# Two operand planes of a two-block model moved by 16 bytes in SBUF: normalised input from 32 to 16 into 256, feed-forward activations from 32 to 48

## The chip, the cores and the metric

One core of a Trainium2 chip runs the whole program; everything is fp32 and enters the matmuls as fp32r (fp32 data that TensorE takes in one pass). The metric is the device time of one execution in microseconds: the median of three runs.

## The reference

Two blocks on 256 tokens of width 1,024, one after the other. In shape:

```python
h = x
h = h + short_conv_mixer(rms_norm(h, ...), ...)                      # 1024 -> 3072 -> 1024
h = h + conv_ffn(rms_norm(h, ffn_norm[0]), w_up, conv_w, w_down)     # first feed-forward
k, v, k_rope = shared_latent_kv(h, ...)
h = h + mla_attention(rms_norm(h, ...), ...)
h = h + conv_ffn(rms_norm(h, ffn_norm[1]), w_up, conv_w, w_down)     # second feed-forward
x = rms_norm(h, final_norm)
# second block: modulated norm, bidirectional gated linear attention with a context
# of 256 tokens, then sqrelu MLP 1024 -> 4096 -> 1024
def conv_ffn(x_n, w_up, conv_w, w_down):                             # d_ff = 2816
    g, u = split(causal_dwconv(x_n @ w_up, conv_w), 2)
    return (silu(g) * u) @ w_down
```

## The kernel before

Activations lie transposed: partitions are 128 features, a chunk of 256 columns is the tokens. A plane such as `xhi` is 8 chunks side by side. For accuracy each operand of a large product is split in two fp32r planes, `hi` (rounded) and `lo` (the rest), and each block of 128x128 weights costs three matmuls of 128x256 into one PSUM bank: `whi` with `hi`, `whi` with `lo`, `wlo` with `hi` (lines L507, L508, L511 of `units`; L486, L487, L490 where a stage follows its input chunk by chunk; L605, L606, L611 for the first two units; L915 to L917 in the linear attention's output).

The weights stream through a ring of four slots of 512 KB: SP loads `raw`, ACT rounds it to `whi` (L1018), DVE subtracts to `wlo` (L1551), PE uses both as the stationary operand. The order is written out by hand for each engine, and semaphores (`slots_done`, `pe_units`, `tile_read`, `x_ready`, `y_ready`) tie them together.

Which plane a stage multiplies:

- `xhi`, `xlo` (one buffer `x2`): the normalised input of the mixer, of both feed-forwards' up projections, of the key/value latents, and of most products of the second block. In its MLP's up projection L510 takes `xhi` and `xlo` in one matmul of 512 columns and L511 follows with 256. In `moving` (L539 to L541) the roles are exchanged: x is stationary, and 512 columns of weights move.
- `yhi`, `ylo`: the mixer's product (8 chunks) and the feed-forwards' activations (22 chunks) before the down projection.
- `mhi`, `mlo`: the MLP's activations; `ohi`, `olo`: attention; `uhi`, `ulo`: four units of the MLP; `zhi`, `zlo`: the modulated context, which is moving operand in one unit (24 matmuls) and stationary in `moving`.

`sb` allocates SBUF buffers one behind another, sizes given in fp32 columns, each rounded up to 32 bytes; `stage.close()` gives the space back to the next buffers. Adding up the sizes, and with the ring at 0 into 256 bytes (`ring_pad` sees to that), the places into 256 are:

| buffer | bytes into 256 |
|---|---|
| raw, whi, wlo | 0 |
| x2 | 32 |
| yhi, ylo, m2, ohi, olo, khi, klo, chi, clo, uhi, ulo, sums_r | 32 |
| zhi, zlo, gates_hi, gates_lo | 0 |
| U | 32 |
| cv, sil, prod, side | 64 |

All these buffers' slices that a matmul reads start whole multiples of 256 bytes further on. `line_pad`, `z_pad` and `sums_pad` hold nothing; `x_held` and `down_held` only keep the space of x2 and of the feed-forward's buffers. `U` holds four results of 256 columns with two zero columns ahead of each, so that DVE's taps of the causal convolution (L1593, L1599) read it at 4 and 0 bytes, and L1695 and L1064 write and read it at 8. ACT writes `xhi` (L1102 and others) and `yhi` (L1060, L1150); DVE writes `xlo` (L1573 and others) and `ylo` (L1687, L1839).

Of the kernel before, what the change touches and what calls it, by code (L numbers as in the profile page):

```python
# [17 lines left out]
F32 = mybir.dt.float32  # L18
F32R = mybir.dt.float32r
# [5 lines left out]
T = 256  # L25
D = 1024
DC = D // P
FF = 2816
FC = FF // P
# [150 lines left out]
def program(nc, stream, xT, ctxT, vec, cst, rot, wa2, crow, out):  # L180
    ctx = ExitStack()

    def sb(name, cols, dt=F32, stack=ctx, rows=P):
        return stack.enter_context(nc.sbuf_tensor(name, [rows, cols], dt))

    with ctx:
# [20 lines left out]
        ee = sb("ee", 4 * GH)  # L207
        state = sb("state", 2 * GH * T)

        sb("line_pad", 32)  # L210
        stage = ExitStack()
        x2 = sb("x2", 2 * DC * T, F32R, stage)
        xhi, xlo = x2[:, 0:DC * T], x2[:, DC * T:2 * DC * T]
        stage.close()
        stage = ExitStack()
        csq_c = sb("csq_c", DC * T, F32, stage)
        stage.close()
        sb("x_held", 2 * DC * T)
        stage = ExitStack()
        yhi = sb("yhi", FC * T, F32R, stage)  # L220
        ylo = sb("ylo", FC * T, F32R, stage)
        U = sb("U", 4 * (T + 2), F32, stage)
        cv = sb("cv", 4 * T, F32, stage)
        sil = sb("sil", 2 * T, F32, stage)
# [2 lines left out]
        stage = ExitStack()  # L227
# [2 lines left out]
        stage.close()  # L230
        EARLY = 2 * HEADS * T + HEADS * T + HP * T + HEADS * T + 2 * T + 2 * D + 4 * RQ * T + 4 * RK * T + 6 * T + 3 * 3 * P + 24
        stage = ExitStack()
        sb("down_held", 2 * FC * T + 4 * (T + 2) + 8 * T, F32, stage)
        side = sb("side", SIDE * D, F32, stage)
        stage.close()
        stage = ExitStack()
# [24 lines left out]
        stage = ExitStack()  # L261
# [8 lines left out]
        stage = ExitStack()  # L270
# [22 lines left out]
        stage = ExitStack()  # L293
# [5 lines left out]
        stage = ExitStack()  # L299
# [2115 lines left out]
```

How the kernel before makes its waits and increments, by code:

```python
    def take(self, sem, by=1):  # L142
        self.n[sem.name] = self.n.get(sem.name, 0) + by
        self.eng.wait_ge(sem, self.value(sem))
# [6 lines left out]
    def again(self, sem, back=0):  # L152
        if self.n.get(sem.name, 0) - back > 0:
            self.eng.wait_ge(sem, self.value(sem, -back))
# [214 lines left out]
        @block.sync  # L370
# [1 line left out]
            def load_group(first, done):  # L372
                for j in range(RING):
                    sp.wait_ge(slots_done, done + (j + 1))
                    sp.dma_start(raw[:, j * D:(j + 1) * D], stream[first + j]).then_inc(raw_ready[j], 16)
# [15 lines left out]
            def load_next(p):  # L391
                sp.wait_ge(slots_done, p - RING + 1)
                sp.dma_start(raw[:, p % RING * D:(p % RING + 1) * D], stream[p]).then_inc(raw_ready[p % RING], 16)
# [11 lines left out]
            def load_down(first, last):  # L405
                for p in range(first, last):
                    load_next(p)
                    kind, u = ORDER[p]
                    if kind == "w" and u in SIDE_BEHIND:
                        s = SIDE_BEHIND[u]
                        if s >= SIDE:
                            sp.wait_ge(side_done, s - SIDE + 1)
                        sp.dma_start(side[:, s % SIDE * D:(s % SIDE + 1) * D], stream[POSITIONS + s])\
                            .then_inc(side_ready[s % SIDE], 16)
# [13 lines left out]
                sp.wait_ge(ev("out_chunk"), n + 1)  # L429
                sp.dma_start(out[:, first * T:last * T], h[:, first * T:last * T]).then_inc(ev("stored"), 16)
            sp.wait_ge(ev("stored"), 16 * len(OUT_PARTS))
```

## Time and profile before

| | |
|---|---|
| median of 3 runs (lowest, highest) | 937.57 us (937.36, 937.75) |
| the profiled execution's own time | 937.42 us |
| its span | 935.6 us, 19,755 instructions |
| PE, weight loads, DVE, ACT busy | 923.4, 879.5, 800.4, 565.6 us |
| granted TensorE clock, mean | 0.997 |
| read from HBM | 193.76 MB, 208 GB/s over the span |

PE stands for the matmuls, PEld for the weight loads that run beside them, DVE and ACT for VectorE and ScalarE; a q behind the name means the engine's sequencer. A matmul's listed duration runs from its start to its modelled end, and the next one starts long before that end: how fast PE works is read from the distance between starts in the timeline.

### The profile page before, as it was taken

The page shows a single profiled execution, that of the slowest core. Times are in us where ns is not written, and L with a number is a line of the kernel's source. Part 1 is how long each engine was busy: PE and PEld are TensorE (multiplying, and loading weights), DVE is VectorE, ACT ScalarE, POOL GpSimd, SP SyncE. Part 2 cuts the span into 40 slices and gives each one's busy share as a digit, 9 for nine tenths or more (in the row PEclk, how much of TensorE's full clock was granted, in tenths as well). Part 3 has the DMA queues.
Part 4 walks back from the last instruction along what each step waited for, and adds up shares of the span by engine and source line. Part 5 has one row for each costly group of instructions (what it writes and reads, how often), then busy time and mean ns, then how long its engine had stood idle before and what let it go on. Part 6 is the DMA issues. An engine that isn't in the chain of part 4 may idle for free.

```text
span 935.6 us, 19755 instructions
## 1 busy us (share of the span) xinstructions
PE 923.4 (99%) x6944; PEld 879.5 (94%) x6944; DVE 800.4 (86%) x1335; ACT 565.6 (60%) x935; POOL 1.8 (0%) x8
## 2 busy tenths in 40 slices
PE   9999999999999999999999999999999999999997
PEld 8999999999999899999999999988899988888886
DVE  6999899999989888899999997956878989886553
ACT  6645666666455566766666555978433667774442
POOL 0000000000000000000000000000000000000000
PEclk9999999999999999999999999999999999999998
DMA  8777575557776555555557765564674348776561
GB/s 298 258 260 231 183 276 200 193 181 275 250 271 215 164 184 173 181 186 196 184 192 274 243 251 187 174 226 157 214 263 154 134 153 265 234 231 222 184 198 45
DMA packets 53877, 195.55 MB, mean 209 GB/s; under 512 B 6110, under 2 KB 6366, under 8 KB 53696
## 3 DMA queue, kind: packets, MB, share of 16 engines
q1 hardware_dynamic: 53680, 193.78, 62.0%
q10 hardware_dynamic: 144, 1.05, 0.3%
q8 instruction: 35, 0.57, 0.2%
q14 instruction: 18, 0.15, 0.0%
HBM read 193.76 MB, written 1.05 MB: 208 GB/s over the span
## 4 chain that ended last, share of the span: by engine, by line
PE 87%; DVE 8%; ACT 2%; issue 1%; DMA 0%; DVEq 0%; SPq 0%; ACTq 0%
PE ps L511 24%; PE ps L507 19%; PE ps L508 19%; PE ps L510 10%; DVE wlo L1551 3%; PE ps L539 1%; PE ps L540 1%; PE ps L541 1%; ACT whi L1018 1%; PE ps L821 1%; DVE a L2040 1%; PE ps L660 1%; PE ps L661 0%; PE ps L662 0%; PE ps L685 0%
## 5 line engine op out<-in xcount | busy, mean ns | idle before, releaser
L1551 DVE TENSOR_TENSOR wlo<-raw,whi 128x1024 fp32r<-128x1024 f32 x303 | 366.7, 1219 | 66.3 <-ACT whi L1018 65.2
L1018 ACT ACTIVATE whi<-raw 128x1024 fp32r<-128x1024 f32 x303 | 316.9, 1052 | 88.4 <-PE ps L511 58.8
L511 PE MATMUL ps<-x,wlo 128*128 128x256 f32 x1288 | 360.0, 280 | 0.0
L507 PE MATMUL ps<-x,whi 128*128 128x256 f32 x1064 | 299.1, 281 | 0.2 <-DVE wlo L1551 0.2
L508 PE MATMUL ps<-x,whi 128*128 128x256 f32 x1064 | 296.9, 279 | 0.0
L511 PEld LDWEIGHTS ps<-x,wlo 128*128 128x128 f32 x1288 | 242.3, 188 | 0.0
L507 PEld LDWEIGHTS ps<-x,whi 128*128 128x128 f32 x1064 | 200.0, 188 | 1.0 <-issue 0.5
L508 PEld LDWEIGHTS ps<-x,whi 128*128 128x128 f32 x1064 | 200.0, 188 | 0.6 <-issue 0.5
L507 PE MATMUL ps<-yhi,whi 128*128 128x256 f32 x400 | 111.6, 279 | 0.0
L511 PE MATMUL ps<-yhi,wlo 128*128 128x256 f32 x400 | 111.6, 279 | 0.0
L508 PE MATMUL ps<-ylo,whi 128*128 128x256 f32 x400 | 111.6, 279 | 0.0
L1064 ACT ACTIVATE cv<-U,vt 128x256 f32<-128x256 f32 x88 | 44.9, 511 | 84.0 <-DVE U L1695 84.0
L510 PE MATMUL ps<-x,whi 128*128 128x512 f32 x224 | 78.1, 391 | 1.1 <-DVE mr L2244 0.7
L510 PE MATMUL ps<-m,whi 128*128 128x512 f32 x224 | 77.7, 390 | 0.0
L507 PEld LDWEIGHTS ps<-yhi,whi 128*128 128x128 f32 x400 | 75.2, 188 | 0.0
L508 PEld LDWEIGHTS ps<-ylo,whi 128*128 128x128 f32 x400 | 75.2, 188 | 0.0
L511 PEld LDWEIGHTS ps<-yhi,wlo 128*128 128x128 f32 x400 | 75.2, 188 | 0.0
L511 PE MATMUL ps<-m,wlo 128*128 128x256 f32 x256 | 72.1, 282 | 0.0
L510 PEld LDWEIGHTS ps<-x,whi 128*128 128x128 f32 x224 | 42.0, 188 | 10.6 <-DVE wlo L1551 1.0
L510 PEld LDWEIGHTS ps<-m,whi 128*128 128x128 f32 x224 | 42.0, 188 | 8.8
L511 PEld LDWEIGHTS ps<-m,wlo 128*128 128x128 f32 x256 | 48.4, 189 | 0.0
L1593 DVE SCALAR_TENSOR_TENSOR cv<-U,vt,cv 128x256 f32<-128x256 f32 x96 | 45.9, 478 | 0.6 <-ACT cv L1164 0.6
(336 smaller groups left out, 1478.9 us busy)
## 6 DMA issues: line engine op xcount, KB each, us to landing
raw<-stream SPq DMA_DIRECT2D x343, 512.0 KB, 4.2
side<-stream SPq DMA_DIRECT2D x16, 512.0 KB, 5.1
h<-xT SPq DMA_DIRECT2D x2, 512.0 KB, 5.9
c<-ctxT ACTq DMA_DIRECT2D x1, 1024.0 KB, 7.0
out<-h SPq DMA_DIRECT2D x4, 256.0 KB, 2.5
ct<-cst SPq DMA_DIRECT2D x1, 898.5 KB
rt_tab<-rot SPq DMA_DIRECT2D x1, 768.0 KB
state<-crow SPq DMA_DIRECT2D x1, 512.0 KB, 6.9
```

The costliest lines, as they stand in the source:

```text
L507: pe.matmul(dst, whi[:, w], at(hi, k), start=(k == 0), stop=False)
L508: pe.matmul(dst, whi[:, w], at(lo, k), start=False, stop=False)
L510: pe.matmul(ps[t % lag][:, :], whi[:, w], halves_of(both, k), start=(k == 0), stop=False)
L511: last = pe.matmul(dst, wlo[:, w], at(hi, k), start=False, stop=(k == K - 1))
L539: pe.matmul(dst, hi[:, tok], whi[:, w], start=first, stop=False)
L540: pe.matmul(dst, lo[:, tok], whi[:, w], start=False, stop=False)
L541: last = pe.matmul(dst, hi[:, tok], wlo[:, w], start=False, stop=final)
L660: pe.matmul(dst, whi[:, w], at(chi, k), start=(k == 0), stop=False)
L1018: c.sig(act.activation(whi[:, s * D:(s + 1) * D], raw[:, r * D:(r + 1) * D], ACT.Copy), hi_ready)
L1064: c.sig(act.activation(at(cv, j), U[:, j * (T + 2) + 2:(j + 1) * (T + 2)], ACT.Copy, scale=vt_col(i * 12 + (base + 3 * j + 2))), tap_ready)
L1551: c.sig(dve.tensor_tensor(wlo[:, w], raw[:, r], whi[:, w], ALU.subtract), slots_done)
L1593: c.sig(dve.scalar_tensor_tensor(out=at(cv, j), in0=U[:, o + 1:o + T + 1], scalar=w1, in1=at(cv, j), op0=ALU.mult, op1=ALU.add), seq_dve)
```

## The change

x2 gets 8 columns more and the program uses it from column 4 on; `line_pad` is 8 columns smaller, so x2's own start falls from 32 to 0 and the planes start at 16. `x_held` is 8 columns larger, so all that follows keeps its place. yhi and ylo become two parts of one buffer y2, used from column 4 on as well: they start at 48. U, cv, sil, prod and side come 32 bytes later. csq_c, which shares x2's space, starts at 0 instead of 32; no matmul reads it as fp32r.

```diff
--- before.py
+++ after.py
@@ -207,18 +207,18 @@
         ee = sb("ee", 4 * GH)
         state = sb("state", 2 * GH * T)
 
-        sb("line_pad", 32)
+        sb("line_pad", 24)
         stage = ExitStack()
-        x2 = sb("x2", 2 * DC * T, F32R, stage)
+        x2 = sb("x2", 2 * DC * T + 8, F32R, stage)[:, 4:4 + 2 * DC * T]
         xhi, xlo = x2[:, 0:DC * T], x2[:, DC * T:2 * DC * T]
         stage.close()
         stage = ExitStack()
         csq_c = sb("csq_c", DC * T, F32, stage)
         stage.close()
-        sb("x_held", 2 * DC * T)
+        sb("x_held", 2 * DC * T + 8)
         stage = ExitStack()
-        yhi = sb("yhi", FC * T, F32R, stage)
-        ylo = sb("ylo", FC * T, F32R, stage)
+        y2 = sb("y2", 2 * FC * T + 8, F32R, stage)[:, 4:4 + 2 * FC * T]
+        yhi, ylo = y2[:, 0:FC * T], y2[:, FC * T:2 * FC * T]
         U = sb("U", 4 * (T + 2), F32, stage)
         cv = sb("cv", 4 * T, F32, stage)
         sil = sb("sil", 2 * T, F32, stage)
@@ -230,7 +230,7 @@
         stage.close()
         EARLY = 2 * HEADS * T + HEADS * T + HP * T + HEADS * T + 2 * T + 2 * D + 4 * RQ * T + 4 * RK * T + 6 * T + 3 * 3 * P + 24
         stage = ExitStack()
-        sb("down_held", 2 * FC * T + 4 * (T + 2) + 8 * T, F32, stage)
+        sb("down_held", 2 * FC * T + 8 + 4 * (T + 2) + 8 * T, F32, stage)
         side = sb("side", SIDE * D, F32, stage)
         stage.close()
         stage = ExitStack()
```

Of the instructions of PE, POOL and SP none moves or changes but for the name y2. On DVE and ACT the residual loops that follow the mixer and the feed-forwards compute the address of x's chunk from a loop counter, and the constant in it is another. On DVE, before (ISA and REGISTER_ALU are register instructions of the sequencer):

```order
113 L145 REGISTER_ALU
114 L1573 ISA
115 L1573 REGISTER_ALU
116 L1573 SCALAR_TENSOR_TENSOR x<-h,vt,x 128x256
117 L1569 TENSOR_TENSOR ssum<-ssum,sq 128x256
118 L145 REGISTER_ALU
119 L1551 TENSOR_TENSOR wlo<-raw,whi 128x1024
```

and now:

```order
113 L145 REGISTER_ALU
114 L1573 ISA x2
115 L1573 SCALAR_TENSOR_TENSOR x<-h,vt,x 128x256
116 L1569 TENSOR_TENSOR ssum<-ssum,sq 128x256
117 L145 REGISTER_ALU
118 L1551 TENSOR_TENSOR wlo<-raw,whi 128x1024
```

The register addition ahead of the subtraction has become a second ISA instruction; the work itself stands in the same order.

## Rows read from the trace of the kernel before

**Rows 1.** The page's first lines: span, then busy us, share and instructions of each engine.

```profile
span 935.6 us, 19755 instructions
...
PE 923.4 (99%) x6944; PEld 879.5 (94%) x6944; DVE 800.4 (86%) x1335; ACT 565.6 (60%) x935; POOL 1.8 (0%) x8
```

**Rows 2.** The page's chain of waits, by engine and by line.

```profile
PE 87%; DVE 8%; ACT 2%; issue 1%; DMA 0%; DVEq 0%; SPq 0%; ACTq 0%
PE ps L511 24%; PE ps L507 19%; PE ps L508 19%; PE ps L510 10%; DVE wlo L1551 3%; PE ps L539 1%; PE ps L540 1%; PE ps L541 1%; ACT whi L1018 1%; PE ps L821 1%; DVE a L2040 1%; PE ps L660 1%; PE ps L661 0%; PE ps L662 0%; PE ps L685 0%
```

**Rows 3.** Groups of PE's instructions: count | busy us, mean ns | idle.

```profile
L511 PE MATMUL ps<-x,wlo 128*128 128x256 f32 x1288 | 360.0, 280 | 0.0
L507 PE MATMUL ps<-x,whi 128*128 128x256 f32 x1064 | 299.1, 281 | 0.2 <-DVE wlo L1551 0.2
L508 PE MATMUL ps<-x,whi 128*128 128x256 f32 x1064 | 296.9, 279 | 0.0
L507 PE MATMUL ps<-yhi,whi 128*128 128x256 f32 x400 | 111.6, 279 | 0.0
...
L510 PE MATMUL ps<-x,whi 128*128 128x512 f32 x224 | 78.1, 391 | 1.1 <-DVE mr L2244 0.7 <-DVE wlo L1551 0.3
...
L539 PE MATMUL ps<-whi,x 128*128 128x512 f32 x32 | 12.7, 398 | 0.0
...
L915 PE MATMUL ps<-x,whi 128*128 128x256 f32 x24 | 7.1, 295 | 0.0
...
L486 PE MATMUL ps<-x,whi 128*128 128x256 f32 x16 | 4.5, 279 | 0.0
...
L605 PE MATMUL ps<-x,whi 128*128 128x256 f32 x16 | 4.3, 300 | 0.0
```

**Rows 4.** Timeline of PE at both ends of an x and a y stretch: start us, length us.

```profile
103.35 0.37 PE L507 MATMUL ps<-x,whi 128*128 128x256 f32 x1
103.56 0.28 PE L508 MATMUL ps<-x,whi 128*128 128x256 f32 x1
...
223.72 0.28 PE L511 MATMUL ps<-x,wlo 128*128 128x256 f32 x1
223.84 0.28 PE L507 MATMUL ps<-yhi,whi 128*128 128x256 f32 x1
...
508.50 0.28 PE L511 MATMUL ps<-x,wlo 128*128 128x256 f32 x1
508.62 0.28 PE L507 MATMUL ps<-yhi,whi 128*128 128x256 f32 x1
```

**Rows 5.** Timeline of PE, from y to z.

```profile
570.10 0.28 PE L511 MATMUL ps<-yhi,wlo 128*128 128x256 f32 x1
570.22 0.28 PE L507 MATMUL ps<-zhi,whi 128*128 128x256 f32 x1
...
570.93 0.28 PE L507 MATMUL ps<-zhi,whi 128*128 128x256 f32 x1
...
572.97 0.28 PE L511 MATMUL ps<-zhi,wlo 128*128 128x256 f32 x1
```

**Rows 6.** Timeline of PE, weights moving: x stationary, then z stationary.

```profile
630.19 0.40 PE L540 MATMUL ps<-whi,x 128*128 128x512 f32 x1
...
632.99 0.40 PE L540 MATMUL ps<-whi,x 128*128 128x512 f32 x1
...
654.94 0.39 PE L539 MATMUL ps<-whi,zhi 128*128 128x512 f32 x1
...
657.66 0.39 PE L539 MATMUL ps<-whi,zhi 128*128 128x512 f32 x1
```

**Rows 7.** Timeline of PE, pairs of 512 and 256 columns: x, then m.

```profile
789.75 0.39 PE L510 MATMUL ps<-x,whi 128*128 128x512 f32 x1
789.98 0.28 PE L511 MATMUL ps<-x,wlo 128*128 128x256 f32 x1
...
791.83 0.39 PE L510 MATMUL ps<-x,whi 128*128 128x512 f32 x1
...
869.83 0.39 PE L510 MATMUL ps<-m,whi 128*128 128x512 f32 x1
...
871.22 0.39 PE L510 MATMUL ps<-m,whi 128*128 128x512 f32 x1
```

**Rows 8.** Groups of DVE and ACT instructions on U, and one of aligned operands.

```profile
L1593 DVE SCALAR_TENSOR_TENSOR cv<-U,vt,cv 128x256 f32<-128x256 f32 x96 | 45.9, 478 | 0.6 <-ACT cv L1164 0.6
L1599 DVE SCALAR_TENSOR_TENSOR cv<-U,vt,cv 128x256 f32<-128x256 f32 x96 | 45.7, 476 | 0.1
...
L1695 DVE TENSOR_TENSOR U<-ps,rstd 128x256 f32<-128x256 f32 x88 | 37.2, 422 | 3.4
L1569 DVE TENSOR_TENSOR ssum<-ssum,sq 128x256 f32<-128x256 f32 x54 | 22.7, 420 | 8.1 <-ACT sq L1027 7.2
...
L1064 ACT ACTIVATE cv<-U,vt 128x256 f32<-128x256 f32 x88 | 44.9, 511 | 84.0 <-DVE U L1695 84.0
...
L1102 ACT ACTIVATE x<-h,vt x24: 493/511/516, 84.7 to 385.2; - x16, 128x256 fp32r<-128x256 f32 x8
```

**Rows 9.** Line L1573: count, duration ns min/median/max.

```profile
L1573 DVEq FUSED_REGOPS  x8: 93/93/99, 85.2 to 101.3; - x8
L1573 DVEq ALU_OP  x2: 40/40/40, 85.4 to 94.7; - x2
```

**Rows 10.** Busy us by stretch: second up and down projections; clock, DMA share, GB/s.

```profile
core 0: us, PE busy (x) PEld busy (x) DVE busy (x) ACT busy (x) POOL busy (x), PEclk, DMA share, GB/s
...
388.00:508.60 120.60, 120.60 (x1035) 120.60 (x1035) 116.60 (x214) 78.41 (x131) 0.00 (x0) 1.00 0.58 198
508.60:570.10 61.50, 61.50 (x529) 61.50 (x528) 55.46 (x87) 35.74 (x51) 0.00 (x0) 1.00 0.73 255
```

## The prediction

> **What bounds the kernel.** I read the profiled execution (937.42 us, of which 935.6 us are the span; the median of the three runs is 937.57 us, 0.15 us above it). The summary of busy time comes first [rows 1]: PE is busy for 923.4 of 935.6 us, DVE for 800.4, ACT for 565.6, and in the stretches used below the granted TensorE clock is 1.00 of the upper of its two levels, 2.4 GHz [rows 10]. The chain of waits [rows 2] then says who sets the end: PE with 87% of the span, of which the four lines that multiply the activation planes by the streamed weights (L511, L507, L508, L510) are 72 points. So what counts is the pace of the matmuls, from one start to the next, and not their listed mean of 280 ns, because each runs into the next one. The groups of PE's instructions [rows 3] give the counts. A 128x256 matmul with plane x as moving operand and a weight tile as stationary one stands at 1,064 times three in the L507, L508 and L511 groups (of the 1,288 of L511, 224 belong to pairs, below); L486 to L490, L605 to L611 and L915 to L917 add 48, 48 and 72 more, one row of each being shown: 3,192 + 168 = 3,360. Plane y has 3 x 400 + 3 x 16 = 1,248.
>
> The timeline gives the pace. In the first feed-forward's up projection, all x, the second matmul starts at 103.56 and the first one on y at 223.84, 1,031 starts later: 120.28 us / 1,031 = **116.7 ns** [rows 4]. In the down projection of the second feed-forward, all y, 527 steps take 570.10 - 508.62 = 61.48 us: again 116.7 ns [rows 4, 5]. At 2.4 GHz that is 280 cycles for 256 columns, 24 of them extra. The change moves only addresses, so the question is whether the pace depends on them. The trace says that it does. All SBUF buffers of this kernel that TensorE streams sit 32 bytes into 256, except the context planes zhi and zlo, which sit at 0. Where PE goes over from y to z at 570.22, with the same weights ring and the same lines, the pace settles at (572.97 - 570.93) / 17 = **120.0 ns** [rows 5], 288 cycles, 32 extra. So 32 bytes (8 columns) of offset in the moving operand took away 8 of 32 extra cycles. With the roles exchanged (activation stationary, weights moving, 512 columns) the sign turns: z at 0 has 2.72 us / 12 = 226.7 ns, x at 32 has 2.80 / 12 = 233.3 ns [rows 6]: 32 extra cycles at 0, 48 at 32. What helps is thus that the moving operand stands further along in its 256 bytes than the stationary one, which is loaded beside it.
>
> **The change, part by part.**
>
> *x from 32 to 16, as moving operand.* No row has a matmul at 16. The nearest are 0 (120.0 ns) and 32 (116.7 ns); it lies midway, and I take the straight line: 118.3 ns, +1.67 ns each. 3,360 x 1.67 = **+5.6 us**. Bounds: as at 0, 3,360 x 3.33 = +11.2 us; as at 32, nothing; and since nothing excludes that 16 is better than 32, the same slope mirrored, -5.6 us.
>
> *x in the pairs.* In the other block's up projection a matmul of 512 columns reads xhi and xlo in one go and one of 256 follows: (791.83 - 789.75) / 6 = 346.7 ns a pair [rows 7], 832 cycles, 64 extra. Of these I count 24 for each of the two instructions, as in the plain ones, and the remaining 16 for the jump between the halves, which the change leaves as it is. 224 pairs [rows 3] x 2 x 1.67 ns = **+0.7 us**, with bounds of 0 and +1.5. The pairs on plane m (347.5 ns, same rows) don't move.
>
> *x as stationary operand.* 96 matmuls (32 on each of L539, L540, L541) [rows 3]. Halfway from 233.3 to 226.7 ns: -3.3 ns each, **-0.3 us**; bounds -0.6 and 0.
>
> *y from 32 to 48.* Outside the two known points. The same line carried on gives 115.0 ns, -1.67 ns x 1,248 = **-2.1 us**. Bounds: 120.0 ns as at 0, +4.2 us; or nothing.
>
> *What lies beside.* ACT and DVE write both planes. Offsets of 4 and 8 bytes occur already in U, whose columns start there: DVE's read one column off takes 478 ns against 476 without, its write two columns off 422 ns against 420 for an aligned sum, ACT's read of U 511 against 511 for x [rows 8]. At most 2 ns on about a hundred instructions an engine, beside PE: nothing. cv, sil, prod and side move by 32 bytes, and none of them is read by TensorE. In the residual loop one DVE register instruction becomes one of the kind that takes 93 ns instead of 40 [rows 9], issued while DVE's previous work still runs; exposed in each of 8 passes it would be 8 x 0.053 = 0.4 us, and I cost it at nothing. No wait, transfer or matmul is added or removed.
>
> *Does PE pass it on?* A slower matmul is passed on in full, since nothing else ends these stretches. A faster one is not quite free: in the up projection DVE is busy for 116.60 of 120.60 us [rows 10], so below a pace of about 113 ns it would be DVE that ends the units. At 115.0 ns PE still needs 118.7 us there. In the down projection DVE needs 55.46 of 61.50 us, so y's gain has room.
>
 The trace does not bear it out as the whole story: z at 0 and x at 32 both begin a 16-byte line, and differ by 3.3 ns.
>
> Sum: 5.6 + 0.7 - 0.3 - 2.1 = +3.9 us on the profiled 937.42: **941.3 us**, 0.4% slower.
>
> **Rivals.**
> *A, the optimum for x lies between 0 and 32 (faster).* The fall from 0 to 32 need not be straight: if it is steep first and rises again past its lowest point, x at 16 gains what I let it lose, and y at 48 loses. Place: the two up projections, 1,032 matmuls each; price -5.6 - 0.7 - 0.3 + 2.1 = -4.5 us: 932.9 us. It decides as soon as x's pace is under 116.7 ns by more than 0.37 of what y's is over it (1,248 / 3,360). For it: two points can't show a curve. Against: all three rows that have an offset follow the order of the straight line. Chance 0.2.
> *B, both gain.* 16 off a multiple of 32 is better on either side of 32: -1.67 x 4,608 - 0.7 - 0.3 = -8.7 us: 928.7 us, less whatever DVE gives back in the up projections. Chance 0.13.
> *C, nothing changes.* Any offset but 0 frees the same 8 cycles, or the new places are worth the same: 937.4 us. For it: y and x at 32 have one pace in every stretch, whatever else runs. Against: 0 and 32 do differ. Chance 0.17. The 16-byte lines of the Trainium skill (above) would give the same 937.4 us.
> *D, both lose.* 32 is a sweet spot and both neighbours lie halfway back to 0 or all the way: +1.67 x 4,608 + 0.7 = +8.4 us, 945.8 us, up to twice that. Chance 0.12.
> That the buffers don't move as said can be left out: the build has the new sizes, and the rest of the layout (m, o, u) stays at 32.
>
> **How the numbers follow.** The straight line has 0.38 and is the likeliest: 941.3 us. Its own range is 938 (x loses a half of the 5.6 us, y gains its 2.1) to 948 (x as bad as at 0, y with nothing to give: +11.2 less 0.6 for x stationary). Over all cases I leave out the lower half of B and the upper part of D and take 930.5 to 948. About 0.2% (1.9 us) is what a measurement of this kernel can tell from no change. Slower: 0.38 + 0.12 = 0.50. Same: 0.17. Faster: 0.20 + 0.13 = 0.33.
>
> **What would show it.** In the changed kernel the up projection's pace (1,031 steps from the second x matmul) should be 118.3 ns, and that stretch 1.7 us longer each time; the down projection's 528 on y should step by 115.0 ns, 0.9 us less each; x's pairs 350 ns; x stationary 230 ns; z, m and the attention's planes unchanged at 120.0, 347.5 and 116.7. x's pace at or below 116.7 ns makes the forecast wrong and leaves A, B or C, which y's pace tells apart; y above 116.7 means A or D. If PE's steps stay as they are and the time still moves, look for DVE's waits at L1573.

## The result, and the profile after

The changed kernel takes **945.42 us** (median of 4 runs, 945.03 to 945.53) against 937.5 us before (937.36 to 937.75): a ratio of 1.0084, 95% interval 1.0072 to 1.0096, or 7.9 us slower where 3.9 were forecast. Its profiled execution took 945.53 us with a span of 943.7 us.

The page of the changed kernel: span, busy time by engine, and the chain of waits by engine and by line.

```profile
span 943.7 us, 19801 instructions
...
PE 931.7 (99%) x6944; PEld 888.8 (94%) x6944; DVE 801.9 (85%) x1335; ACT 565.5 (60%) x935; POOL 1.8 (0%) x8
...
PE 91%; DVE 6%; ACT 2%; issue 1%; DMA 0%; DVEq 0%; SPq 0%; ACTq 0%
PE ps L511 25%; PE ps L507 20%; PE ps L508 19%; PE ps L510 10%; DVE wlo L1551 2%; PE ps L539 2%; PE ps L541 1%; PE ps L540 1%; PE ps L821 1%; ACT whi L1018 1%; PE ps L660 1%; PE ps L661 0%; PE ps L662 0%; DMA h<-xT 0%; PE ps L685 0%
```

PE is busy 8.3 us longer, with the same 6,944 matmuls as in [rows 1], and the span is 8.1 us longer; DVE adds 1.5 us, ACT nothing. PE's share of the chain rises from 87% [rows 2] to 91%. The matmuls became slower, and nothing else took their place.

The timeline of PE in the changed kernel, at the same places as [rows 4, 5]: second x matmul and first y matmul of the first feed-forward, then first and last matmul of the second one's down projection.

```profile
104.92 0.28 PE L508 MATMUL ps<-x,whi 128*128 128x256 f32 x1
...
227.26 0.28 PE L507 MATMUL ps<-y,whi 128*128 128x256 f32 x1
...
515.07 0.28 PE L507 MATMUL ps<-y,whi 128*128 128x256 f32 x1
...
577.43 0.28 PE L511 MATMUL ps<-y,wlo 128*128 128x256 f32 x1
```

x: (227.26 - 104.92) us / 1,031 = 118.7 ns, where it was 116.7; 118.3 was forecast. y: (577.43 - 515.07) us / 527 = 118.3 ns, where it was 116.7 too; 115.0 was forecast. In cycles of 2.4 GHz, 280 has become 285 for x and 284 for y.

The same timeline where x is used otherwise, and on z: z as moving operand, x's pairs, x as stationary operand.

```profile
578.02 0.28 PE L508 MATMUL ps<-zlo,whi 128*128 128x256 f32 x1
...
580.30 0.28 PE L511 MATMUL ps<-zhi,wlo 128*128 128x256 f32 x1
...
799.86 0.39 PE L510 MATMUL ps<-x,whi 128*128 128x512 f32 x1
...
801.94 0.39 PE L510 MATMUL ps<-x,whi 128*128 128x512 f32 x1
...
636.87 0.39 PE L540 MATMUL ps<-whi,x 128*128 128x512 f32 x1
...
639.67 0.39 PE L540 MATMUL ps<-whi,x 128*128 128x512 f32 x1
```

z: 2.28 us / 19 = 120.0 ns, as before. Pairs: 2.08 us / 6 = 346.7 ns, as in [rows 7], where 350 was forecast. x stationary: 2.80 us / 12 = 233.3 ns, as in [rows 6], where 230 was forecast.

The two projections of the second feed-forward, busy us of each engine, to set against [rows 10].

```profile
core 0: us, PE busy (x) PEld busy (x) DVE busy (x) ACT busy (x) POOL busy (x), PEclk, DMA share, GB/s
392.50:515.00 122.50, 122.50 (x1034) 122.50 (x1034) 117.04 (x214) 78.42 (x131) 0.00 (x0) 1.00 0.59 195
515.07:577.50 62.43, 62.43 (x530) 62.43 (x529) 55.66 (x87) 35.69 (x51) 0.00 (x0) 1.00 0.73 251
```

From start to start (the windows of [rows 10] begin 0.1 us early) the up projection is 2.1 us longer and the down projection 0.9 us, with DVE's work in them within 0.5 us of what it was (117.04 and 55.66 us).

Groups of DVE's instructions on U, which now stands at 64, and on ssum, which has not moved.

```profile
L1593 DVE SCALAR_TENSOR_TENSOR cv<-U,vt,cv 128x256 f32<-128x256 f32 x96 | 46.1, 480 | 0.6 <-ACT cv L1164 0.6
...
L1695 DVE TENSOR_TENSOR U<-ps,rstd 128x256 f32<-128x256 f32 x88 | 37.3, 424 | 6.7 <-PE ps L511 5.2
L1569 DVE TENSOR_TENSOR ssum<-ssum,sq 128x256 f32<-128x256 f32 x54 | 22.8, 422 | 8.1 <-ACT sq L1027 7.2
```

The register instructions of L1573, duration ns min/median/max.

```profile
L1573 DVEq FUSED_REGOPS  x16: 53/79/99, 86.2 to 102.7; - x16
```

480, 424 and 422 ns against 478, 422 and 420 [rows 8]: 2 ns on each, on the aligned sum as well. The register instructions are 16 where there were 10 [rows 9], and beside DVE's work.

Stretch by stretch from the timelines of both kernels: x's stretches are 5.5 us longer in all (twice 2.1 in the up projections, 1.0 in the mixer's input, the rest in pieces of 24 to 156 matmuls), y's are 2.1 us longer (0.3 + 0.9 + 0.9). That is 7.6 of the 8.1 us of span; another 0.4 us lies in the last 6 us, behind the last product of the MLP, and its cause is open. x does not have one pace here: in the single units of 24 matmuls of the second block it runs at 116.7 to 116.8 ns at its new place too, which is why x costs 5.5 us and not 3,360 x 2.0 = 6.7.

### The profile page after: what moved, and what is told of

It reads as the page before. It is cut to its first block, busy times and chain, and to the rows that moved or that the text cites. A ratio compares the mean times of both kernels' runs of the same rounds, so it can differ in the third digit from the quotient of the medians.

```text
span 943.7 us, 19801 instructions
## 1 busy us (share of the span) xinstructions
PE 931.7 (99%) x6944; PEld 888.8 (94%) x6944; DVE 801.9 (85%) x1335; ACT 565.5 (60%) x935; POOL 1.8 (0%) x8
## 4 chain that ended last, share of the span: by engine, by line
PE 91%; DVE 6%; ACT 2%; issue 1%; DMA 0%; DVEq 0%; SPq 0%; ACTq 0%
PE ps L511 25%; PE ps L507 20%; PE ps L508 19%; PE ps L510 10%; DVE wlo L1551 2%; PE ps L539 2%; PE ps L541 1%; PE ps L540 1%; PE ps L821 1%; ACT whi L1018 1%; PE ps L660 1%; PE ps L661 0%; PE ps L662 0%; DMA h<-xT 0%; PE ps L685 0%
## 5 line engine op out<-in xcount | busy, mean ns | idle before, releaser
L508 PE MATMUL ps<-y,whi 128*128 128x256 f32 x400 | 112.4, 281 | 0.0
L511 PE MATMUL ps<-y,wlo 128*128 128x256 f32 x400 | 112.4, 281 | 0.0
L507 PE MATMUL ps<-y,whi 128*128 128x256 f32 x400 | 112.3, 281 | 0.0
L511 PEld LDWEIGHTS ps<-y,wlo 128*128 128x128 f32 x400 | 75.2, 188 | 0.0
L507 PEld LDWEIGHTS ps<-y,whi 128*128 128x128 f32 x400 | 75.2, 188 | 0.0
L508 PEld LDWEIGHTS ps<-y,whi 128*128 128x128 f32 x400 | 75.2, 188 | 0.0
```

Of the source, the lines that this page charges most:

```text
L507: pe.matmul(dst, whi[:, w], at(hi, k), start=(k == 0), stop=False)
L508: pe.matmul(dst, whi[:, w], at(lo, k), start=False, stop=False)
L511: last = pe.matmul(dst, wlo[:, w], at(hi, k), start=False, stop=(k == K - 1))
```

## The experiments

All kernels of a group ran on one chip with runs of the kernel before beside them; the medians are over all runs of each.

### One plane at a time

x at 16 alone:

```diff
-        sb("line_pad", 32)
+        sb("line_pad", 24)
...
-        x2 = sb("x2", 2 * DC * T, F32R, stage)
+        x2 = sb("x2", 2 * DC * T + 8, F32R, stage)[:, 4:4 + 2 * DC * T]
...
-        sb("x_held", 2 * DC * T)
+        sb("x_held", 2 * DC * T + 8)
```

> Only x's part of the change: x at 16 into 256, y back at 32. The changed kernel's own timeline gave 118.7 ns from start to start on plain x matmuls (285 cycles) and 118.3 ns on y, against 116.7 ns for both before. If the two planes act independently, this kernel is slower than the one before by about 3,360 x 2.0 = 6.7 us less what the few stretches with other waits hide, so about 943.5 to 944.2 us, with x at 118.7 ns and y at 116.7 ns. If instead the cost came from U, cv, sil and prod standing 32 bytes later (a rival), or from the two planes being apart, the time is back at 937.5 us.

Measured 943.16 us against 937.77 (ratio 1.0051, 1.0034 to 1.0068): +5.4 us, 0.3 us under the expected 943.5. The timeline of PE: second x matmul of the second up projection, then first and last y matmul of the down projection.

```profile
391.65 0.28 PE L508 MATMUL ps<-x,whi 128*128 128x256 f32 x1
...
514.00 0.28 PE L507 MATMUL ps<-yhi,whi 128*128 128x256 f32 x1
...
575.48 0.28 PE L511 MATMUL ps<-yhi,wlo 128*128 128x256 f32 x1
```

x: 122.35 us / 1,031 = 118.7 ns, and the same in the first up projection; y: 61.48 us / 527 = 116.7 ns. The rival is out: with U, cv, sil and prod where they were, x's part of the cost is there.

y at 48 alone:

```diff
-        yhi = sb("yhi", FC * T, F32R, stage)
-        ylo = sb("ylo", FC * T, F32R, stage)
+        y2 = sb("y2", 2 * FC * T + 8, F32R, stage)[:, 4:4 + 2 * FC * T]
+        yhi, ylo = y2[:, 0:FC * T], y2[:, FC * T:2 * FC * T]
...
-        sb("down_held", 2 * FC * T + 4 * (T + 2) + 8 * T, F32, stage)
+        sb("down_held", 2 * FC * T + 8 + 4 * (T + 2) + 8 * T, F32, stage)
```

> Only y's part of the change: y at 48, U, cv, sil, prod and side 32 bytes later, x at 32. If the planes act independently: 1,248 x 1.67 = 2.1 us slower, 939.6 us, y at 118.3 ns and x at 116.7 ns. If U's shift is what costs, x's stretches (where U, cv, sil and prod are worked on) slow down here and not in the run with x at 16.

Measured 940.93 us against 937.77 (ratio 1.003, 1.0018 to 1.0041): +3.2 us, 1.1 more than expected. The timeline of PE tells where that is: second x matmul and last x matmul of the first up projection, then second x matmul of the second one and the first y matmul behind it.

```profile
104.11 0.28 PE L508 MATMUL ps<-x,whi 128*128 128x256 f32 x1
...
225.42 0.28 PE L511 MATMUL ps<-x,wlo 128*128 128x256 f32 x1
...
391.06 0.28 PE L508 MATMUL ps<-x,whi 128*128 128x256 f32 x1
...
511.35 0.28 PE L507 MATMUL ps<-y,whi 128*128 128x256 f32 x1
```

y is at 118.3 ns as expected. But x, which this kernel does not touch, runs at (225.42 - 104.11) us / 1,030 = **117.8 ns** in the first up projection and at (511.35 - 391.06) us / 1,031 = 116.7 ns in the second. The same buffers, the same instructions, two paces, each held for a thousand matmuls. That was the first sign that a place does not have one pace. Both planes alone add up to 5.4 + 3.2 = 8.6 us, against 7.9 together; this stretch's 1.1 us are more than the difference.

### The mirror image

x at 48, y at 16; the rooms are 64 columns larger so that all else keeps its place into 256.

```diff
-        x2 = sb("x2", 2 * DC * T, F32R, stage)
+        x2 = sb("x2", 2 * DC * T + 64, F32R, stage)[:, 4:4 + 2 * DC * T]
...
+        y2 = sb("y2", 2 * FC * T + 64, F32R, stage)[:, 60:60 + 2 * FC * T]
```

> The mirror image: x at 48, y at 16, all other buffers where they were into 256. Theory 1 (what costs is to stand an odd number of 16-byte steps off, whichever side of 32): x 118.3 to 118.7 ns and y the same, so the same time as the changed kernel, 945.4 us. Theory 2 (the straight line of the prediction with a bend: every step away from 0 helps, and 48 was bad for y for another reason): x at 48 at or below 116.7 ns and y at 16 at 118.3 to 118.7 ns, 939.5 us or less. Theory 3 (the distance to 32 counts, symmetric): not told from theory 1 here, but the table of offsets tells it.

Measured 943.19 us against 937.77 (ratio 1.0059, 1.004 to 1.0079). The timeline of PE at the same places:

```profile
390.90 0.28 PE L508 MATMUL ps<-x,whi 128*128 128x256 f32 x1
...
512.90 0.28 PE L507 MATMUL ps<-y,whi 128*128 128x256 f32 x1
...
574.38 0.28 PE L511 MATMUL ps<-y,wlo 128*128 128x256 f32 x1
```

Neither theory holds whole: x at 48 takes 122.00 us / 1,031 = 118.3 ns, as in all its long stretches, the same as y at 48; y at 16 takes 61.48 us / 527 = 116.7 ns, as in both down projections, where x at 16 had 118.7. In the mixer's output of the same kernel, 192 matmuls, y at 16 settles at 285 cycles all the same. The straight line of the prediction is out (48 is worse than 32 for x as well), and so is "an odd number of 16-byte steps costs".

### The pace by itself: tables of offsets

The tables leave the model out altogether: fp32r matmuls alone, in the order whi, whi, wlo against hi, lo, hi. Their times as kernels mean nothing. The loop of the second table, without its lines for the pairs:

```diff
+            def run(mm, base, lo, chunks, both=False, os=0):
...
+                for i in range(N):
+                    k, r = i // 3 % chunks, i % 3
...
+                    at = base + k * T + (lo if r == 1 else 0)
+                    w = weights((wh, wh, wl)[r], i // 3, os)
...
+                        mm(dst[:, 0:T], w, mv[:, at:at + T], start=first, stop=last)
```

> A table of the pace by itself: no model, only runs of 60 fp32r matmuls each, in the order whi, whi, wlo against hi, lo, hi, with the moving operand at 18 places into 256 (stationary at 0), the stationary at 6 places (moving at 32), and some of both; 256 columns, and 512 columns for eight of them. The output is the input x, nothing of the model is computed. All theories expect 288 cycles (120.0 ns) for moving 0 and 280 (116.7 ns) for moving 32 with the stationary at 0. Theory 1 (odd 16-byte steps cost): 16, 48, 80, 112 alike at 284 to 285 cycles, 32, 64, 96 alike at 280 or less. Theory 2 (straight line): 284 at 16, 276 at 48, falling on. Theory 3 (distance to 32 modulo 64): 284 at 16 and 48, 288 at 64 and 128, 280 at 96 and 160. Theory 4 (what counts is the distance between the moving and the stationary operand): moving 48 with stationary 16 and moving 64 with stationary 32 are the same as moving 32 with stationary 0; if instead each one's own place counts, they differ.

The first table has hi and lo, and whi and wlo, 4,352 bytes apart. Moving 0 gave 288 cycles and 32 gave 282.7, but 16 gave 280, 48 gave 284, and neither a straight line nor a bend at 32 came out: 64, 112 and 192 gave **272**, and 80 and 96 gave 288. A moving operand 4 bytes off gave the worst value of all, 296. The timeline of this table at place 4, first and last of 24 steps, then 512 contiguous columns at moving 32, the same:

```profile
33.09 0.29 PE L70 MATMUL ps<-mh,wl 128*128 128x256 f32 x1
...
36.05 0.29 PE L70 MATMUL ps<-mh,wl 128*128 128x256 f32 x1
...
262.85 0.40 PE L100 MATMUL ps<-mh,wl 128*128 128x512 f32 x1
...
268.45 0.40 PE L100 MATMUL ps<-mh,wl 128*128 128x512 f32 x1
```

2.96 us / 24 = 123.3 ns, 296 cycles; 5.60 us / 24 = 233.3 ns, 560 cycles, where 512 columns with both operands at 0 took 544. The second table has the addresses of this kernel.

> Again no model, only matmuls (the output is the input x): runs of 48, now at exactly the addresses of this kernel (weights in the ring's whi and wlo, moving operand in x2's and y's space, hi and lo as far apart as there), with x at 64 places 16 bytes apart over 1,024 bytes, y at 16 places over 256, and the pairs of 512 and 256 columns at 16 places. The first table, with hi and lo 4,352 bytes apart, gave 280 cycles at 16, 282.5 at 32 and 284 at 48, while the model shows 285 for x at 16 and 280 at 32. Theory 1 (the pace is set by where each stream stands against the other, hi and lo included, and by nothing else that runs): this table gives x 280 at 32, 285 at 16, 284 at 48, y 280 at 32 and 280 to 281 at 16, 284 at 48, as the kernels did, and repeats every 256 bytes. Theory 2 (ACT's and DVE's accesses beside the matmuls set it): the table differs from the kernels. If the dips of the first table (272 cycles at 64, 112 and 192) are there again, a version with x and y at one of them is faster than both kernels by up to 8 cycles x 4,608 = 15 us, unless DVE, 97% busy in the up projections, ends them at 113.0 ns a matmul.

Cycles from start to start, mean of the last 24 of 48 matmuls (of the last 8 of 16 pairs), by bytes into 256:

```
place    0      16     32     48     64     80     96     112
x        288.0  285.0  280.0  284.0  282.6  288.0  288.0  272.0
y        288.0  284.9  280.0  284.0  282.6  288.0  288.0  272.0
pair     832    832    832    842    846    848    840    848

place    128    144    160    176    192    208    224    240
x        284.5  285.2  281.6  286.4  272.0  286.0  284.0  281.5
y        284.5  285.2  281.7  286.4  272.0  286.0  284.0  281.5
pair     841    848    832    840    848    840    832    848
```

The other 48 places of x (up to 1,008 bytes) repeat this row to within 0.1 cycle: the period is 256 bytes. Theory 1 holds but for one number: no other engine works in these stretches, and the table has the 285 of x at 16, the 284 at 48, the 280 at 32, the 288 of z at 0, and the unchanged 832 of the pairs at 16. For y at 16 it has 284.9, where the mirrored kernel's down projections ran at 280. The timeline of this table at x's places 32 and 112, each the first and last of 24 steps:

```profile
39.51 0.28 PE L82 MATMUL ps<-mv,wl 128*128 128x256 f32 x1
...
42.31 0.28 PE L82 MATMUL ps<-mv,wl 128*128 128x256 f32 x1
...
67.89 0.28 PE L87 MATMUL ps<-mv,wl 128*128 128x256 f32 x1
...
70.61 0.28 PE L87 MATMUL ps<-mv,wl 128*128 128x256 f32 x1
```

2.80 us / 24 = 116.7 ns, and 2.72 us / 24 = 113.3 ns. The row is no line and no valley: 32 is a local low point with 16 and 48 above it on either side.

What was open was why y at 16 ran at 280 in a kernel and x at 32 at 282.6 in one stretch. The third table enters each place from each of seven, and after one or three fp32 matmuls.

> The open point: y at 16 ran at 280 cycles in the mirrored kernel and the first table had 280 at 16, while the changed kernel's x at 16 and the second table have 285, and one late stretch of the kernel with x at 16 alone ran at 288. No model, matmuls alone (output is the input x): every one of 7 places (0, 16, 32, 48, 64, 112, 192), 48 matmuls each, entered from each of the 7 and after one or three fp32 matmuls. Theory 1 (the pace is fixed by the place): each place has one value whatever came before. Theory 2 (the streams lock into one of several patterns and stay there): places 16 and 64 show two values or more, such as 280 and 285, 272 and 282.6, depending on what ran before, and 0, 32, 112 and 192 show one.

Cycles reached, by what ran just before:

```
place      from 0   16     32     48     64         112    192    1 fp32  3 fp32
0          288      288    288    288    288        288    288    288     288
16         285      285    280    272    285, 280   285    280    280     280
32         283      280    280    283, 280  280     280    280    280     283
48         284      284    284    284    284        284    284    284     284
64         283    283, 272 283, 272 283, 272  272   283    283    283     283
112        272      272    272    272    272        272    272    272     272
192        272      283    272    272    272        272    272    283     272
```

Theory 2 holds, more strongly than expected: 32 and 192 have two paces as well. The timeline of this table at place 16, entered from 0, from 32 and from 48, first and last of 24 steps each:

```profile
40.56 0.28 PE L86 MATMUL ps<-mv,wl 128*128 128x256 f32 x1
...
43.41 0.28 PE L86 MATMUL ps<-mv,wl 128*128 128x256 f32 x1
...
150.36 0.28 PE L107 MATMUL ps<-mv,wl 128*128 128x256 f32 x1
...
153.16 0.28 PE L107 MATMUL ps<-mv,wl 128*128 128x256 f32 x1
...
161.57 0.28 PE L109 MATMUL ps<-mv,wl 128*128 128x256 f32 x1
...
164.29 0.28 PE L109 MATMUL ps<-mv,wl 128*128 128x256 f32 x1
```

2.85, 2.80 and 2.72 us for the same 24 steps of the same instructions on the same addresses: 118.7, 116.7 and 113.3 ns. Once in a pattern the stream stays in it for the 24 steps measured. Only 0, 48 and 112 had one pace in every entry. Two values in one field mean that the place just before does not settle the pace: 16 was entered from 64 twice, both times with 64 at 282.7 cycles, and ran at 285 once and at 280 once.

> No model (output is the input x). 48 matmuls at each of 16 places of the moving operand, now for six places of the stationary one (0, 16, 32, 64, 112, 128), each entered after three fp32 matmuls. Theory 1: only the distance between moving and stationary operand counts: the row for stationary 16 is that for 0 shifted by 16, with its 272s at 128 and 208. Theory 2: each operand's own place counts (the line it starts in): the 272s stay at 112 and 192, or go. The first table spoke for distance with exceptions: (16,16) was 284 and (0,0) and (32,32) 288, (48,16) 284 and (32,0) 280 to 282.6.

The fourth table moved the stationary operand too (each entry after three fp32 matmuls). With the stationary at 32 and 64 the 272 of place 112 is found again at 144 and 176, and at 64 that of 192 is at 0; with the stationary at 128 they are at 240 and 64. With the stationary at 16 there is one 272, at 208, and at 112 one, at 48 (304 less 256): the distance of 192 keeps it, and the distance of 112 gives 288 and 284 there. So for steps of 32 bytes of the stationary operand the 272 of a distance of 112 goes with the distance, as theory 1 has it, and with the stationary at 16 or 112 its own place counts as well. Theory 1 is not shown whole: with the stationary at 0, 32, 64 and 128 a distance of 80 gave 288, 284, 288 and 284, one of 128 gave 284.5, 288, 284.5 and 288, and one of 192 gave 282.6, 282.7, 272 and 272. For 192 the last table has both values as states of one place; whether the others are states too was not tried.

### Places that the table calls fast

```diff
-        x2 = sb("x2", 2 * DC * T, F32R, stage)
+        x2 = sb("x2", 2 * DC * T + 64, F32R, stage)[:, 40:40 + 2 * DC * T]
...
+        y2 = sb("y2", 2 * FC * T + 64, F32R, stage)[:, 40:40 + 2 * FC * T]
```

> x and y both at 192 into 256, all else where it was. The table at this kernel's addresses gives 272 cycles (113.3 ns) there against 280 (116.7 ns) at 32, and the pairs 848 against 832. If the table holds in the kernel: 4,608 x 3.33 = 15.4 us less, plus 224 x 6.7 = 1.5 us for the pairs: about 924 us. DVE is the limit on that: it is busy 116.6 of 120.6 us in an up projection, and at 113.3 ns PE would take 117.0 us, so part of the two up projections' 3.4 us each may come back as waits for DVE, and the time be up to 930 us. A rival: in the kernel the pace is held at 280 by something that the table lacks (ACT and DVE beside it), and the time stays at 937.5 us or rises.

Measured 941.7 us against 937.72 (ratio 1.0034, 1.0023 to 1.0045): a miss, 4 us slower where up to 15 less were expected. The timeline of its first up projection, second and last x matmul:

```profile
104.15 0.28 PE L508 MATMUL ps<-x,whi 128*128 128x256 f32 x1
...
225.46 0.28 PE L511 MATMUL ps<-x,wlo 128*128 128x256 f32 x1
```

121.31 us / 1,030 = 117.8 ns, which is the other state of 192 (282.7 cycles), and both up and both down projections sit in it. Shorter pieces of x in the same kernel, the 156 matmuls ahead of the MLP among them, settle at 272. Two of the eight executions took 939.3 and 939.4 us, the other six 941.4 to 942.3, so a stretch may also fall in another state from one execution to the next; with one trace that isn't shown. y at 192 alone:

> Only y at 192, x at 32. 1,248 x 3.33 = 4.2 us less: 933.4 us, with the down projections at 113.3 ns a matmul (DVE has 55.5 of 61.5 us to do there, so it is not in the way). If planes act independently, what x at 192 brings is the difference to the run with both.

Measured 935.75 us against 937.72 (ratio 0.998, 0.9971 to 0.999), 2.0 us less where 4.2 were expected. The timeline of PE at the first and last y matmul of each down projection:

```profile
223.34 0.28 PE L507 MATMUL ps<-y,whi 128*128 128x256 f32 x1
...
283.12 0.28 PE L511 MATMUL ps<-y,wlo 128*128 128x256 f32 x1
...
506.40 0.28 PE L507 MATMUL ps<-y,whi 128*128 128x256 f32 x1
...
568.30 0.28 PE L511 MATMUL ps<-y,wlo 128*128 128x256 f32 x1
```

The first took 59.78 us / 527 = 113.4 ns and the second 61.90 us / 527 = 117.5 ns: both states in one kernel.

The same with 20 in place of 40 puts both planes at 112.

> x and y both at 112 into 256, an odd number of 16-byte steps. The table gives 272 cycles, as at 192, and the pairs 848. If only the table's value counts: the same time as with both at 192. If an odd multiple of 16 costs DVE or ACT something when they write and read x and y, their groups on x and y are longer here than at 192 and the time is some us more.

Measured **927.28 us** against 937.72 (ratio 0.989, 0.9873 to 0.9906), between the 924 and the 930 us that were expected of both planes at 272. The timeline of its second up projection, second x matmul and first y matmul:

```profile
381.39 0.28 PE L508 MATMUL ps<-x,whi 128*128 128x256 f32 x1
...
498.27 0.28 PE L507 MATMUL ps<-y,whi 128*128 128x256 f32 x1
```

116.88 us / 1,031 = 113.4 ns. The same stretches as [rows 10], busy us:

```profile
core 0: us, PE busy (x) PEld busy (x) DVE busy (x) ACT busy (x) POOL busy (x), PEclk, DMA share, GB/s
381.40:498.30 116.90, 116.90 (x1033) 116.90 (x1033) 114.70 (x214) 78.48 (x131) 0.00 (x0) 1.00 0.61 203
498.40:558.70 60.30, 60.14 (x529) 59.87 (x528) 55.28 (x87) 35.39 (x51) 0.00 (x0) 1.00 0.74 256
```

DVE is busy for 114.70 of 116.90 us there and PE for all of it, so DVE does not end the units yet; in the down projection PE idles for 0.16 us in 60.30. An odd multiple of 16 bytes costs DVE and ACT nothing to speak of: DVE's group that writes ylo (L1687) takes 420 ns an instruction against 419 at 32 and at 192, and the busy times of DVE and ACT are 795.7 and 565.2 us, under the 800.4 and 565.6 of [rows 1]. What this version pays is in the pairs, 178.3 ns a step against 175.3, as the table said (848 against 832).

```diff
+        x2, x2m = x2[:, 20:20 + 2 * DC * T], x2[:, 0:2 * DC * T]
+        xhim, xlom = x2m[:, 0:DC * T], x2m[:, DC * T:2 * DC * T]
...
-            units(MC - 4, DC, xhi, xlo, both=x2)
+            units(MC - 4, DC, xhim, xlom, both=x2m)
```

> x and y at 112 as in the run that took 927.3 us, but the second block's MLP writes and reads its normalised input 80 bytes lower in the same buffer, at 32. Its pairs took 349.8 ns at 112 against 346.5 ns at 32 by the two stretches of 447 steps (178.34 and 175.3 ns a step): 447 x 3.0 = 1.35 us less, so 925.9 us. If the time stays at 927.3, the pairs' loss was hidden.

Measured **925.12 us** against 937.84 (ratio 0.9874, 0.9857 to 0.989): the pairs are back at 175.3 ns a step. The medians differ by 2.2 us where 1.35 was expected; the two kernels ran in different groups. Of the 2.3 us between their two traces 1.3 lie in the stretch of the pairs, the rest mostly in the first units and behind the MLP, for which the edit gives no reason. Its page:

```profile
span 923.1 us, 19801 instructions
...
PE 910.1 (99%) x6944; PEld 866.3 (94%) x6944; DVE 795.9 (86%) x1335; ACT 565.1 (61%) x935; POOL 1.8 (0%) x8
...
PE 84%; DVE 11%; ACT 2%; issue 2%; DVEq 0%; ACTq 0%
PE ps L513 23%; PE ps L509 18%; PE ps L510 17%; PE ps L512 10%; DVE wlo L1553 4%; PE ps L541 1%; PE ps L543 1%; PE ps L542 1%; ACT whi L1020 1%; PE ps L620 1%; PE ps L823 1%; DVE a L2042 1%; PE ps L662 1%; PE ps L663 1%; PE ps L664 1%
```

PE is busy for 13.3 us less than in [rows 1] with the same matmuls, and its share of the chain is down from 87% [rows 2] to 84%, DVE's up from 8% to 11%: DVE is probably what this version will meet next.

```diff
-        ohi = sb("ohi", HEADS * T, F32R, stage)
-        olo = sb("olo", HEADS * T, F32R, stage)
+        o2 = sb("o2", 2 * HEADS * T + 64, F32R, stage)[:, 20:20 + 2 * HEADS * T]
+        ohi, olo = o2[:, 0:HEADS * T], o2[:, HEADS * T:2 * HEADS * T]
```

> As the run before it, and attention's planes ohi and olo at 112 too. 288 matmuls x 3.33 ns = 0.96 us if all of them run at PE's pace; the stretches on o stand at 120.7 ns a matmul and contain waits, so between 0 and 1 us less, 925 to 926 us. If it is slower, a plane used in pieces is caught in another state.

Measured 924.97 us against 937.84 (ratio 0.9864, 0.9848 to 0.9881). Against the run before it this is inside the noise; the long stretch on o went from 120.8 to 120.0 ns a matmul, which is 0.1 us.

## Why the prediction was right and wrong

- *What bounds the kernel.* Right: PE ends every stretch that matters, the pace of its matmuls depends on where the operands stand into 256 bytes, and a slower pace was passed on in full.
- *x as moving operand, +5.6 us.* Right in sign and in size: +5.5 us by the stretches, +5.4 us alone. The size is luck: the long stretches lost 2.0 ns a matmul, more than the 1.67 of the line, and the single units of the second block lost nothing. The reason was wrong: 285 cycles at 16 is not midway on a line from 288 to 280; from another start the same place gives 280 or 272.
- *y to 48, -2.1 us.* **This is the step that failed**: "the same line carried on gives 115.0 ns". Measured 118.3 ns, +2.1 us: y at 48 is slower than at 32, and there is no line. This term is 4.2 us off, as much as the sum, which is 4.1 us off; the pairs (-0.7), x stationary (+0.3), x (-0.1) and the 0.4 us behind the MLP nearly cancel. The bounds of this term, -2.1 to +4.2, did contain it.
- *"What helps is thus that the moving operand stands further along in its 256 bytes than the stationary one".* Wrong, and it spoke for carrying the line on past 32. In its rows the activation moved with 256 columns and the weights with 512, and it laid the change of sign to the roles. The first table has both orders at both widths: with 512 columns moving, 32 against 0 takes 560 cycles and 0 against 0 takes 544, so there the moving operand further along is slower; with 256 columns, moving 0 against stationary 32 takes 284, faster than the 288 of 0 against 0.
- *Pairs, +0.7 us, and x stationary, -0.3 us.* Both nothing. The first was put together from a count of extra cycles per instruction; the table has 832 at 0, 16 and 32. The second interpolated between two rows and found 233.3 ns again: with 512 contiguous columns moving, the first table has 556 to 560 cycles for all seven pairings of places other than 0 with 0, which has 544.
- *ACT, DVE and the register instructions at nothing.* Right: 2 ns an instruction, off the path.
- *The rivals.* D, "both lose, both neighbours halfway back to 0", with 945.8 us, is what happened in its outcome (285 and 284 of 280 to 288). Its picture, a sweet spot with slopes, is wrong too: 16 from 48 had 272. A, B and C are out for this kernel. The rule of 16-byte lines (the Trainium skill, SBUF - State Buffer, section "SBUF: two separate sides") would have given no change; the table disagrees, since its 16 places all begin such a line and run from 272 to 288 cycles. Of the places inside a line, 4 is slower than all of them (296) and 8 is not (281.3).
- *What should have been seen.* Two values of the offset cannot carry a straight line, let alone one extended past them, and z's pace came from a single unit of 24 matmuls. The honest term for y was the range of its bounds; D deserved more than 0.12.

What remains open is the mechanism behind the numbers: why 112 and 192 are 8 cycles below 32, why a stream keeps the pattern in which it was caught, and which pattern a given entry in the kernel leads to. xy192 shows that the tables don't foretell that where a place has more than one state. The tables show that no other engine is needed for several states; whether ACT's and DVE's work has a part in which one a stretch of the kernel falls into was not tried. It was not tried whether a short run of other matmuls ahead of a long stretch moves it into a faster state.

## What to carry to other kernels

Where TensorE's stream of matmuls is the bound, measure the distance from start to start by the place of the moving operand into 256 bytes against the stationary one, at 16-byte steps, in a small kernel of matmuls alone and at the real distances between planes; a pair of planes read in one matmul, or an operand used as stationary, has a table of its own. Enter each place from several others, and take one that has a single fast value (here 112) over one that has it only sometimes (192, 64): both planes at 112 made the whole kernel 1.1% faster for some columns of padding, both at 192 made it 0.3% slower, and 64 was not tried in a kernel. The kernel's own timeline has to confirm the pace. And don't interpolate an alignment effect: its neighbours say nothing.

## What the runs showed of the hardware that was not expected

- 128x256 fp32r matmuls with a new weight tile each run at 272 to 288 cycles (113.3 to 120.0 ns) by the places of their operands at 16-byte steps, with no other engine at work; the row repeats every 256 bytes. At 4 bytes they take 296.
- The pace has several steady states at one place (16: 272, 280, 285; 64: 272, 283; 32: 280, 283; 192: 272, 283). Which one comes changes with what ran before, though the run just before does not settle it, and one is kept for over a thousand matmuls in this kernel. In the kernel with x at 16 alone, the last 135 steps ahead of the MLP ran at a fourth, 288 (16.20 us).
- With the stationary operand at 0, 32, 64 and 128 the distance of 112 between the two operands gives 272; with it at 16 or 112 that distance gives 288 and 284, and the distance of 192 gives 272.
